# Prompt attention of a hybrid decoder step: the selected and the window branch of a head as one unit for the first two query blocks

## The reference

```
s_s = einsum('bqgrd,bqgkcd->bqgrkc', q, kb) * scale
p_s = masked_softmax(s_s.reshape(b, nq, g, r, nk), m_s)
o_s = einsum('bqgrkc,bqgkcd->bqgrd', p_s, vb)
s_w = einsum('bqgrd,bkgd->bqgrk', q, kw) * scale
p_w = masked_softmax(s_w, m_w)
o_w = einsum('bqgrk,bkgd->bqgrd', p_w, vw)
return gate[..., 0:1] * o_c + gate[..., 1:2] * o_s + gate[..., 2:3] * o_w
```

## Time and profile before

| what | value |
|---|---|
| median of three executions | 1498.16 us (1494.76 to 1498.63) |
| profiled execution, its own time | 1490.45 us |
| its span | 1488.8 us |
| TensorE busy | 1460.0 us, 98% of the span |
| VectorE, ScalarE, GpSimd busy | 845.7, 414.2, 189.2 us |
| the attention stage | from 684.7 us to about 804 us of the span |

### The profile page before, as it was taken

One profiled execution on the slowest core, in us unless ns is written; L12 is line 12 of the kernel. 1 busy time (PEld: TensorE's weight loads), 2 busy tenths in 40 slices (PEclk: granted clock), 3 DMA queues, 4 the chain that ended last, 5 costly groups with the idle time before them and its releaser, 6 DMA issues.

```text
span 1488.8 us, 30697 instructions
## 1 busy us (share of the span) xinstructions
PE 1460.0 (98%) x12466; PEld 1140.7 (77%) x12466; DVE 845.7 (57%) x1703; ACT 414.2 (28%) x900; POOL 189.2 (13%) x256
## 2 busy tenths in 40 slices
PE   9999999999999999999999989999999999999997
PEld 8887578777777776886667758888788888888886
DVE  7655058633343346415776346676666666666664
ACT  3112362123233215116776541102211110110101
POOL 1000324432122213204000410000000000000000
PEclk9999999999999999999999999999999999999999
DMA  6222543211111238447100975332222222222221
GB/s 260 86 85 71 181 161 125 79 47 49 42 47 45 88 123 257 165 132 219 45 2 2 289 275 225 135 99 85 71 85 86 85 83 75 84 85 86 97 87 60
DMA packets 57400, 163.96 MB, mean 110 GB/s; under 512 B 7312, under 2 KB 19696, under 8 KB 55952
## 3 DMA queue, kind: packets, MB, share of 16 engines
q1 hardware_dynamic: 48608, 121.46, 24.7%
q0 software_dynamic: 7936, 39.40, 7.6%
q10 hardware_dynamic: 720, 1.16, 0.2%
HBM read 144.01 MB, written 22.15 MB: 112 GB/s over the span
## 4 chain that ended last, share of the span: by engine, by line
PE 95%; DVE 3%; issue 1%; ACT 1%; DMA 0%; SPq 0%; DVEq 0%; ACTq 0%
PE acc L1040 26%; PE acc L1187 14%; PE acc L1953 5%; PE acc L1981 5%; PE acc L1962 5%; PE acc L1212 5%; PE acc L2006 3%; PE acc L1707 2%; PE acc L1731 2%; PE acc L1135 2%; PE acc L1323 2%; PE acc L1720 2%; PE acc L1150 2%; PE acc L1340 1%; PE acc L1052 1%; PE acc L1075 1%
## 5 line engine op out<-in xcount | busy, mean ns | idle before, releaser
L1040 PE MATMUL acc<-sb_work,sb_ring 128*128 128x272 f32 x602 | 150.9, 393 | 0.0
L2488 ACT ACTIVATE sb_omemT<-acc 128x272 f32<-128x272 f32 x74 | 29.3, 396 | 386.0 <-PE acc L1953 234.2
L1040 PE MATMUL acc<-sb_work 128*128 128x272 f32 x530 | 133.1, 393 | 0.0
L1040 PEld LDWEIGHTS acc<-sb_work,sb_ring 128*128 128x128 f32 x602 | 114.7, 190 | 23.3
L1040 PEld LDWEIGHTS acc<-sb_work 128*128 128x128 f32 x530 | 100.8, 190 | 21.2 <-issue 0.8
L1187 PE MATMUL acc<-sb_work,sb_ring 128*128 128x272 f32 x360 | 100.8, 409 | 0.6 <-DVE sb_work L2691 0.6
L1953 PE MATMUL acc<-sb_work,sb_ring 128*128 128x272 f32 x308 | 77.2, 393 | 1.0 <-issue 1.0
L1212 PE MATMUL acc<-sb_work,sb_ring 128*128 128x272 f32 x320 | 77.7, 396 | 0.0
L1962 PE MATMUL acc<-sb_work,sb_ring 128*128 128x272 f32 x308 | 77.1, 393 | 0.0
L1187 PEld LDWEIGHTS acc<-sb_work,sb_ring 128*128 128x128 f32 x360 | 63.8, 190 | 14.7 <-issue 1.7
L1212 PEld LDWEIGHTS acc<-sb_work,sb_ring 128*128 128x128 f32 x320 | 59.8, 190 | 14.7 <-issue 3.3
(11 more groups left out here) (488 smaller groups left out, 2805.8 us busy)
## 6 DMA issues: line engine op xcount, KB each, us to landing
sb_ring<-w_stream SPq DMA_DIRECT2D x144, 512.0 KB, 3.5
sb_work<-pages SPq DMA_DIRECT2D x56, 192.0 KB, 4.2
branch_gates<-sb_work SPq DMA_DIRECT2D x24, 272.0 KB, 2.5
sb_work<-branch_gates POOLq DMA_DIRECT2D x8, 816.0 KB, 15.0
sb_ring<-w_stream SPq DMA_DIRECT2D x16, 384.0 KB, 3.5
sb_work<-mem_kT SPq DMA_DIRECT2D x8, 512.0 KB, 8.1
sb_work<-mem_v SPq DMA_DIRECT2D x8, 512.0 KB, 10.7
query_features<-sb_work SPq DMA_DIRECT2D x10, 272.0 KB, 3.8
```

The costliest lines, as they stand in the source:

```text
L1040: mm = pe.matmul(out, w[:, q, :], x[q], start=q == 0, stop=q == n - 1)
```

## The change

For blocks 0 and 1, where both branches together have no more than 512 keys a group (one PSUM bank), the two branches become one unit: their scores stand side by side, one product for each group reads both key tiles (which lie two tiles apart), one mask product covers both diagonals, one reduction gives all four maxima. The exponentials stay one for each group and branch. The scaling of such a unit is one tensor_tensor with the four factors spread over their keys, in place of the tensor_scalars. Blocks 2 and 3 stay one unit for each branch. So there are 36 units, six a head, and the semaphore counts follow; the small factors take sixteen columns with two places in turn; `att_out` comes at one turn in six.

```diff
-        ATT_UNITS = [(r, t, b) for r in range(HPG) for t in range(QT) for b in range(2)]
+        ATT_UNITS = [(r, t, bs) for r in range(HPG) for t in range(QT)
+                     for bs in ((range(2),) if 2 * (t + 1) * P <= 512 else (range(1), range(1, 2)))]
+        HEAD_UNITS = N_ATT // HPG
+        T_ATT = (T_SK, T_WK)
...
             def att_scores(u):
+                o = acc[u % 2][:, :, 0:nb * w].rearrange("p g (b k) -> p g b k", b=nb)
                 for g in range(NG):
-                    pe.matmul(acc[u % 2][:, g, 0:w], qT[gs, r, t * P:w], in_all[gs, (T_SK, T_WK)[b], 0:w],
-                              start=True, stop=False)
+                    keys = in_all[gs, T_ATT[bs[0]]:T_ATT[bs[-1]] + 1:T_WK - T_SK, 0:w]
+                    pe.matmul(o[:, g], qT[gs, r, t * P:w], keys, start=True, stop=False)
                 for g in range(NG):
-                    mm = pe.matmul(acc[u % 2][:, g, t * P:w], bf_ident, bf_causal, start=False, stop=True)
+                    mm = pe.matmul(o[:, g, :, t * P:w], bf_ident, bc(bf_causal, 1, nb), start=False, stop=True)
...
             def att_turn(u):
-                    for k in range(t + 1):
+                    for k in range(len(bs) * (t + 1)):
...
             def att_values(u):
-                for k in range(t + 1):
+                for n, (b, k) in enumerate((b, k) for b in bs for k in range(t + 1)):
...
             def att_exp(u):
                 for g in range(NG):
-                    ins = act.activation(probs[u % 3][:, g, 0:w], acc[u % 2][:, g, 0:w], ACT.Exp,
-                                         bias=small[:, c + g:c + g + 1], accum_out=small[:, c + 2 + g:c + 3 + g])
+                    for n in range(nb):
+                        at_, keys = c + g * nb + n, slice(n * w, (n + 1) * w)
+                        ins = act.activation(probs[u % 3][:, g, keys], acc[u % 2][:, g, keys], ACT.Exp,
+                                             bias=small[:, at_:at_ + 1], accum_out=small[:, at_ + 4:at_ + 5])
...
             def att_copy(u):
-                act.activation(probsT[:, u % 2, :, 0:(t + 1) * P], acc[2][:, :, 0:(t + 1) * P], ACT.Copy).then_inc(at_copied, 1)
+                act.activation(probsT[:, u % 2, :, 0:n], acc[2][:, :, 0:n], ACT.Copy).then_inc(at_copied, 1)
...
             def att_max(u):
-                dve.tensor_reduce(small[:, c:c + 2], acc[u % 2][:, :, 0:(t + 1) * P], AX, ALU.max, negate=True)\
+                dve.tensor_reduce(small[:, c:c + 2 * nb].rearrange("p (g b) -> p g b", g=NG),
+                                  acc[u % 2][:, :, 0:nb * w].rearrange("p g (b k) -> p g b k", b=nb), AX, ALU.max, negate=True)\
...
             def att_scale(u):
+                if nb == 2:
+                    shown = probs[u % 3][:, :, 0:nb * w].rearrange("p g (b k) -> p g b k", b=nb)
+                    ins = dve.tensor_tensor(shown, shown, bc(rows(12).rearrange("p (g b) -> p g b", g=NG), 3, w), ALU.mult)
+                else:
+                    for g in range(NG):
+                        ins = dve.tensor_scalar(probs[u % 3][:, g, 0:w], probs[u % 3][:, g, 0:w],
+                                                small[:, c + 12 + g:c + 13 + g], None, ALU.mult)
...
             def att_out(r):
-                dve.wait_ge(at_pv, 2 * QT * (r + 1))
+                dve.wait_ge(at_pv, HEAD_UNITS * (r + 1))
...
-                if u >= 5 and (u - 5) % (2 * QT) == 2 * QT - 1:
-                    att_out((u - 5) // (2 * QT))
+                if u >= 5 and (u - 5) % HEAD_UNITS == HEAD_UNITS - 1:
+                    att_out((u - 5) // HEAD_UNITS)
```

More of the change, by code:

```diff
@@ L1699, in att_scores @@
             def att_scores(u):
-                r, t, b = ATT_UNITS[u]
-                w = (t + 1) * P
+                r, t, bs = ATT_UNITS[u]
+                w, nb = (t + 1) * P, len(bs)
                 if u >= 2:
@@ L1723, in att_values @@
             def att_values(u):
-                r, t, b = ATT_UNITS[u]
+                r, t, bs = ATT_UNITS[u]
                 pe.wait_ge(at_copied, u + 1)
-                if t == 0 and b == 0 and r >= 2:
+                if t == 0 and r >= 2:
                     pe.wait_ge(at_o, r - 1)
                 settle()
-                for k in range(t + 1):
+                for n, (b, k) in enumerate((b, k) for b in bs for k in range(t + 1)):
                     for g in range(NG):
                         mm = pe.matmul(acc[3][g * HD:(g + 1) * HD, r % 2, t * P:(t + 1) * P],
-                                       v_tm[:, b, k, g * HD:(g + 1) * HD], probsT[:, u % 2, g, k * P:(k + 1) * P],
+                                       v_tm[:, b, k, g * HD:(g + 1) * HD], probsT[:, u % 2, g, n * P:(n + 1) * P],
                                        start=b == 0 and k == 0, stop=b == 1 and k == t, skip_group_check=True)
@@ L2354, in att_exp @@
             def att_exp(u):
-                r, t, b = ATT_UNITS[u]
-                w, c = (t + 1) * P, 8 * (u % 4)
+                r, t, bs = ATT_UNITS[u]
+                w, nb, c = (t + 1) * P, len(bs), 16 * (u % 2)
                 act.wait_ge(at_max, u + 1)
@@ L2360, in att_exp @@
                 for g in range(NG):
-                    ins = act.activation(probs[u % 3][:, g, 0:w], acc[u % 2][:, g, 0:w], ACT.Exp,
-                                         bias=small[:, c + g:c + g + 1], accum_out=small[:, c + 2 + g:c + 3 + g])
+                    for n in range(nb):
+                        at_, keys = c + g * nb + n, slice(n * w, (n + 1) * w)
+                        ins = act.activation(probs[u % 3][:, g, keys], acc[u % 2][:, g, keys], ACT.Exp,
+                                             bias=small[:, at_:at_ + 1], accum_out=small[:, at_ + 4:at_ + 5])
                 ins.then_inc(at_exp, 1)
             def att_copy(u):
-                r, t, b = ATT_UNITS[u]
+                r, t, bs = ATT_UNITS[u]
+                n = len(bs) * (t + 1) * P
                 act.wait_ge(at_turn, u + 1)
@@ L2945, in att_max @@
             def att_max(u):
-                r, t, b = ATT_UNITS[u]
-                c = 8 * (u % 4)
+                r, t, bs = ATT_UNITS[u]
+                w, nb, c = (t + 1) * P, len(bs), 16 * (u % 2)
                 dve.wait_ge(at_s, u + 1)
-                dve.tensor_reduce(small[:, c:c + 2], acc[u % 2][:, :, 0:(t + 1) * P], AX, ALU.max, negate=True)\
+                dve.tensor_reduce(small[:, c:c + 2 * nb].rearrange("p (g b) -> p g b", g=NG),
+                                  acc[u % 2][:, :, 0:nb * w].rearrange("p g (b k) -> p g b k", b=nb), AX, ALU.max, negate=True)\
@@ L2950, in att_max @@
                    .then_inc(at_max, 1)
             def att_scale(u):
-                r, t, b = ATT_UNITS[u]
-                w, c = (t + 1) * P, 8 * (u % 4)
+                r, t, bs = ATT_UNITS[u]
+                w, nb, c = (t + 1) * P, len(bs), 16 * (u % 2)
+                rows = lambda n: small[:, c + n:c + n + NG * nb]
+                gates = gates_tm[:, t, :].rearrange("p (g r b) -> p g r b", g=NG, b=3)[:, :, r, 1 + bs[0]:2 + bs[-1]]
                 dve.wait_ge(at_exp, u + 1)
-                own(dve.reciprocal(small[:, c + 4:c + 6], small[:, c + 2:c + 4]))
@@ L2957, in att_scale @@
[L2957 to L2961, removed]
+                own(dve.reciprocal(rows(8), rows(4)))
+                own(dve.tensor_tensor(rows(12).rearrange("p (g b) -> p g b", g=NG),
+                                      rows(8).rearrange("p (g b) -> p g b", g=NG), gates, ALU.mult))
```

2 lines of the change are left out of this document (1 added, 1 removed).

## The result

The kernel with the change takes 1482.2 us, the median of eight executions (1480.97 to 1489.89). The kernel before, run beside it, takes 1493.94 us over eight (1490.58 to 1498.63). The ratio is 0.992, with a 95% interval from 0.9899 to 0.994: faster by about 12 us, 9 to 15. The miss of 8.7 us has two parts of like size: the base 1498.16 was 4.2 us above the median that eight executions give, and the gain is 11.7 us where 7.3 was forecast.

A forecast was written before the change was run, and what follows sets the result against it. TensorE, busy nearly the whole span, was taken as the bound. Five heads at 1.51 us less 0.18 for the first give 7.4, taken as 7.3: from the median 1498.16, 1490.9 us (range 1486 to 1496.5).

The forecast's parts named there:

- the base: Starting time for the forecast: median 1498.16 us of the runs shown, 7.7 us above the profiled execution.
- the stalls: TensorE's waits before transposes in the attention stage: 0.54 us a head instead of 1.13.
- T(2): Transposes of a block 2 unit: VectorE's chain 2.10 us against 2.53 of TensorE work, so no wait.
- T(3): Transposes of a block 3 unit: 0.28 us lost instead of 0.61; idle time before them about 0.1.
- T(1): Transposes of the joined block 1 unit: 0.26 us lost through VectorE; the way through ScalarE, 0.17, covered by that.
- The first head: Attention stage's start: bigger units fill the pipeline, so this head loses 0.18 us where it would gain 0.92.
- S(3): Scores of a block 3 unit, with mask; before, in the first head, they start 9.67 us after the first scores.
- ScalarE's order eats part: Rival, attention stage: copy, exponentials and scaling run 0.6 us longer, gain only 4.3 us, 1493.9 us; chance 0.14.
- merging saves no TensorE work: Rival, attention stage: only columns count, so just less stall is gained, 1.8 us, 1496.4 us; chance 0.05.
- stalls vanish: Rival, attention stage: another 0.2 to 0.5 us a head, gain 9 to 10 us, 1488.5 us; chance 0.06.
- The slower one: Rival, attention stage: block 1's unit keeps its PSUM pair too long, delaying later scores; 1502.7 us; chance 0.03.
- After the stage: Behind the attention stage: later loads move forward with its end, no transfer swallows the gain, no new DMA or semaphore.

The follow-up runs named there:

- the pair with the store held: Kernels before and after, each with GpSimd's cmp_w1 loads held back until the branch_gates stores landed: 1492.77 us and 1481.84 us.
- block 1 alone: Changed kernel with only block 1's two branches joined in one unit, block 0 left split: 1495.66 us, ratio 1.0004 to the kernel before.

## Why the prediction was right and where it failed

**What was right.** The stage. TensorE's work a head was put at 16.76 us, the stalls at 0.54, the period at 17.30: the period is 17.28. The joined scores were expected at 0.63 and 1.06 and are 0.63 and 1.06; the joined values 0.59 and 1.03, and are that; the mask pair 0.34 against 0.33; the scaling of block 0 0.69 and of block 1 1.225, against means of 692 and 1224 ns in the groups of VectorE:

```profile
L2971 DVE TENSOR_TENSOR sb_omemT<-sb_omemT,sb_small 128x1024 f32<-128x1024 f32 x6 | 7.3, 1224 | 0.2
...
L2971 DVE TENSOR_TENSOR sb_omemT<-sb_omemT,sb_small 128x512 f32<-128x512 f32 x6 | 4.2, 692 | 0.2
```

The exponentials of the first joined unit take 1.50 us against 1.48. T(2) waits no longer, as computed. T(3) has 0.35 us of idle time where "about 0.1" was said, T(1) 0.23: together 0.58 beside the 0.54, with a split that is a little off. The first head behaves as worked out: S(3) begins 9.34 us after the first scores (694.30 to 703.64), where the sum had 9.41 (684.73 to 694.14). The stage is 7.5 us shorter, for 7.3 to 7.4 forecast.

**The rivals.** That ScalarE's order eats part fell: no transposes wait for the way through ScalarE, though it stays near (in the period shown its last exponential for T(1) is done at 717.43 us, VectorE's maximum at 717.65). That merging saves no TensorE work fell: the period would be 18.2 by it. That stalls vanish fell too: two stay. The measured gain of 11.7 us is nearer to that last rival's 9 to 10 than to 7.3, but by accident, since the further gain is elsewhere. The slower one has nothing for it.

**The step that failed** is "After the stage", with its sign "the stage's end about 7.3 us earlier and the rest unmoved": the sum has no term for the stretches behind the stage. I had looked there for transfers and semaphores that the change could touch, and it touches none. It shortens TensorE's instruction queue by 180 instructions, and the queue itself has places where the engine stops while DMA is full. The stops moved, and by their new places and the clock behind them they cost some 3.5 us less in the samples' stretch (69.6 to 66.1, and 71.0 to 67.3 in the pair with the store held). Of that 0.9 is given back behind it, where TensorE waits for the weights' load that lands later. The net is 2.8 us in the pair with the store held, of 4.4 us missing in the first comparison; the other 1.6 are within what eight executions of each can tell.

**The second failure is the base.** The forecast was moved from the profiled 1490.45 to the median of three, 1498.16. The text saw the distance of 7.7 us and did not ask for its cause. By their times two of these three executions, 1498.63 and 1498.16, were of the slower group, which goes with the late store; eight executions give 1493.94. Without moving it, 1490.45 - 7.3 = 1483.2 stood in the text, 1.0 us from the result. That would have been luck: the profiled execution is 3.5 us under the median of eight, and this happens to stand in for the gain behind the stage. From 1493.94 the same sum gives 1486.6.

**What stays open.** That the stops come at fixed distances of instructions is shown. That the next block of instructions is late because the DMA engines are full fits the traces (a packet of the instruction queue that starts only inside the stop; as many instructions without a stop where the DMA share is 0.00), but no run empties the engines at the places of the stops. Why the weights' load behind the samples takes longer, and what the 0.17 us before each block are, is not known. And one cannot say that the 2.8 us belong to the change as a rule: another edit of the same size elsewhere would have moved the stops as well.

## What to carry to other kernels

In a long program that one engine bounds, an edit that changes the number of instructions on that engine moves the places behind it where the queue stops; compare the stretches that the edit does not touch as well, before the whole difference is put down to the edit. When the profiled execution is further from the median than the gain in question, find out first what separates them, and forecast by differences between executions of one group. Joining units pays where a block has a fixed cost on the bounding engine, but joining one size of unit can rob the next of its cover: here block 1 alone gave nothing, and with block 0 it takes another 1.4 us off the stage.

## What the runs showed of the hardware

- TensorE's instruction stream stops it: 0.8 to 3.5 us at a time, about 127 matmul records apart, where matmuls are short (1.80 us for 117 of them) and the DMA share is 1.03; in 4.43 us with as many instructions and a share of 0.00 it doesn't. Moving the queue by 76 or by 180 instructions puts the stops of one kernel where the other has them, and 76 + 180 is 256, so the places repeat after 256 instructions (127 records are 254 of them, waits and increments the others). In the page of the kernel before, the instruction queue has packets of 16.4 KB each:

```profile
q8 instruction: 100, 1.64, 0.4%
```

  The Trainium skill ("Runtime: NRT & Kernel Launch", "Instruction fetch mechanics") has instructions fetched in blocks of 16 KiB, 256 instructions, which agrees with both numbers; it calls the cost of crossing a block "mostly hidden", and here stops of up to 3.24 us are not.
- After some of these stops, and after some waits of 4.9 us and more, the granted clock is at its lower level (1.2 GHz) for 3.4 to 10.2 us, so a stop can cost more than its length: 3.18 us instead of 1.86 for L1856 behind the stops of 1.76 and 3.24 us. After 1.52 and 1.37 us it stays at 1.00.
- Stores of 272 KB issued near 559 us took 11.6 to 18.9 us while GpSimd's loads of 1 MB each were under way; with these held back to about 569 us they took 6.5 to 7.8, and ScalarE's wait was gone.
- An empty semaphore increment costs 0.15 us at the start of TensorE's queue (76 in 11.2 us, 180 in 27.0), and nothing that shows in front of the stage's scores and values (a period of 17.28 us with and without).
